# Two residual blocks on one core: projection, norm and transposes chained per block of 128 tokens

## What is computed

```python
h = rmsnorm(x, norm_g)            # before each L1 layer
proj = h @ w_in
...
x = x + u @ w_o                   # end of each L1 layer
# second kind, twice:
h = rmsnorm_2(x, g_mix[l]);  proj = h @ w_in;  ...;  x = x + merged @ w_out[l]
h = rmsnorm_2(x, g_mlp[l]);  up = square(relu(h @ w_up[l]));  x = x + up @ w_down[l]
# at the end
return rmsnorm_2(x, g_final)
```

## Time and profile before

| | us |
|---|---|
| median of 3 runs (3376.45 to 3382.3) | 3376.96 |
| the profiled execution's own time | 3382.91 |
| span of that execution, first to last instruction | 3381.1 |
| PE matmul busy | 3251.9 (96%) |
| DVE / ACT / POOL busy | 1437.8 / 820.0 / 1821.1 |
| mean granted TensorE clock | 0.986 |

### The profile page before, as it was taken

One profiled execution on the slowest core, in us unless ns is written; L12 is line 12 of the kernel. 1 busy time (PEld: TensorE's weight loads), 2 busy tenths in 40 slices (PEclk: granted clock), 3 DMA queues, 4 the chain that ended last, 5 costly groups with the idle time before them and its releaser, 6 DMA issues.

```text
span 3381.1 us, 47060 instructions
## 1 busy us (share of the span) xinstructions
PE 3251.9 (96%) x15456; PEld 2691.9 (80%) x15456; DVE 1437.8 (43%) x2325; ACT 820.0 (24%) x1773; POOL 1821.1 (54%) x1028
## 2 busy tenths in 40 slices
PE   5998999998998999999999999999899999999998
PEld 4877888886777888878887887888788888878887
DVE  7777462117776642126666112111166662121011
ACT  4554332014554331022222002101122220021020
POOL 3444455663444555655455665666554555656664
PEclk9999999999999999999999999999999999999999
DMA  3222222222221222232222222222222222222322
GB/s 106 75 89 67 69 75 81 98 98 63 87 87 57 76 73 89 98 102 84 75 84 78 90 96 88 94 99 95 83 84 84 75 83 87 99 87 94 99 93 99
DMA packets 87983, 290.54 MB, mean 86 GB/s; under 512 B 12833, under 2 KB 13537, under 8 KB 87921
## 3 DMA queue, kind: packets, MB, share of 16 engines
q1 hardware_dynamic: 75024, 273.12, 24.3%
q10 hardware_dynamic: 12896, 16.64, 1.8%
HBM read 275.00 MB, written 2.10 MB: 82 GB/s over the span
## 4 chain that ended last, share of the span: by engine, by line
PE 87%; DVE 7%; issue 3%; ACT 1%; ACTq 1%; DVEq 0%; DMA 0%
PE bank L556 27%; PE bank L558 27%; PE bank L557 27%; PE bank L624 1%; DVE xq L1416 1%; PE bank L742 1%; PE bank L605 1%; PE bank L653 1%; DVE k_hi L1347 1%; ACTq L1032 1%; PE bank L775 1%; DVE xk L1416 1%; DVE xn L1356 0%; DVE xk L1412 0%; PE bank L715 0%
## 5 line engine op out<-in xcount | busy, mean ns | idle before, releaser
L537 POOL TENSOR_SCALAR w_hi<-raw 128x1024 fp32r<-128x1024 f32 x512 | 560.6, 1095 | 1493.7 <-DMA raw<-in_w_in 1026.9
L540 POOL TENSOR_TENSOR w_lo<-raw,w_hi 128x1024 fp32r<-128x1024 f32 x512 | 1260.4, 2462 | 42.7
L556 PE MATMUL bank<-h_lo,w_hi 128*128 128x512 f32 x2816 | 1118.4, 397 | 0.6 <-DVE h_lo L1359 0.3
L558 PE MATMUL bank<-h_hi,w_hi 128*128 128x512 f32 x2816 | 1099.9, 391 | 0.0
L557 PE MATMUL bank<-h_hi,w_lo 128*128 128x512 f32 x2816 | 1098.7, 390 | 0.0
L558 PEld LDWEIGHTS bank<-h_hi,w_hi 128*128 128x128 f32 x2816 | 530.4, 188 | 113.2
L556 PEld LDWEIGHTS bank<-h_lo,w_hi 128*128 128x128 f32 x2816 | 531.4, 189 | 108.8 <-issue 2.5
L557 PEld LDWEIGHTS bank<-h_hi,w_lo 128*128 128x128 f32 x2816 | 531.6, 189 | 106.0
L1373 DVE TENSOR_TENSOR x<-x,bank 128x512 f32 x64 | 44.0, 688 | 458.1 <-PE bank L558 458.1
L556 PE MATMUL bank<-w_lo,up_hi 128*128 128x512 f32 x512 | 199.2, 389 | 0.0
L557 PE MATMUL bank<-w_hi,up_lo 128*128 128x512 f32 x512 | 199.2, 389 | 0.0
(11 more groups left out here) (297 smaller groups left out, 4520.1 us busy)
## 6 DMA issues: line engine op xcount, KB each, us to landing
raw<-in_w_in SPq DMA_DIRECT2D x288, 512.0 KB, 3.3
raw<-in_w_up SPq DMA_DIRECT2D x64, 512.0 KB, 3.3
raw<-in_w_down SPq DMA_DIRECT2D x64, 512.0 KB, 3.2
raw<-in_w_out_a SPq DMA_DIRECT2D x16, 512.0 KB, 3.2
raw<-in_w_out_b SPq DMA_DIRECT2D x16, 512.0 KB, 3.3
raw<-in_w_o SPq DMA_DIRECT2D x16, 512.0 KB, 3.2
raw<-in_p_ret SPq DMA_DIRECT2D x16, 512.0 KB, 3.3
raw<-in_p_sb SPq DMA_DIRECT2D x16, 512.0 KB, 3.3
```

Of the source, the lines that this page charges most:

```text
L537: nc.gpsimd.tensor_scalar(m.w_hi[:, slot], m.raw[:, slot], 1.0, 0.0, ALU.mult, ALU.add).then_inc(s["w_step"], 1)
L540: nc.gpsimd.tensor_tensor(m.w_lo[:, slot], m.raw[:, slot], m.w_hi[:, slot].bitcast(F32), ALU.subtract).then_inc(s["split"], 1)
L556: nc.tensor.matmul(dst, hi, rhs_lo, start=first, stop=False, **more)
L558: return nc.tensor.matmul(dst, hi, rhs_hi, start=False, stop=last, **more)
```

## The change

1. `project` keeps the panels' order for all but the last three (`HELD = 3`) and does these three sorted by block: block 0 of the three panels, block 1, and so on. The two column halves are written out, and in the second half of a projection that a norm follows, PE transposes block 0 (8 transposes) behind the matmuls of block 1, and block 1 behind those of block 2. `used` for the three panels is given only in the last block.
2. `first_panels` replaces the first two gemms of the next stage: transposes of block 2; first panel, tokens 0 to 255; transposes of block 3; second panel, tokens 0 to 255; then tokens 256 to 511 of both. Matmuls have 256 moving columns there, 96 in place of 48.
3. The gain is now multiplied in along the row: DVE's `normalised(b)` is a `scalar_tensor_tensor` of `x`, the root and `g_row` (128x1024, a 512 KB broadcast load for each norm). `h_high` and `h_low` work on one block of tokens, 8 steps of 128x512 as before. `xn` moves away from `u_hi`/`u_lo`.
4. The norm stands at the end of a loop turn instead of the start on ACT and DVE, so `layer_parameters` and the rotation tables of L2 are now issued behind the norm. PE's turn begins with `first_panels`.
5. At the start SP loads `x` without waiting, and the norm of the input goes ahead of the sine and cosine, the parameters and the masks.
6. PE's loops over `R_HEADS` and over the two MLP halves are partly written out, with the same work.
7. After the last projection PE still transposes all four blocks and ACT and DVE still split them, though nothing reads that.

```diff
+HELD = 3
-        place = Region(nc, o_u, o_rest)
+        place = Region(nc, o_u + 2 * tile, o_rest)
         self.xn = place.put("xn", [P, TB, D])
@@ tensor
+            def first_panels():
+                slots = [(at.n.get("panel", 0) + i) % RING for i in range(2)]
+                banks = [acc[(at.n.get("acc", 0) + i) % 2] for i in range(2)]
...
+                early, late = slice(0, 2 * P), slice(2 * P, S)
+                turn_block(2)
+                pe.wait_ge(s["split"], at.at("panel", 1))
+                pe.wait_ge(acc_free[at.n.get("acc", 0) % 2], at.at("acc", 2, div=2))
+                pe.wait_ge(s["h_ready"], at.at("norm", times=KT) + TB)
+                half(0, early)
+                turn_block(3)
+                pe.wait_ge(s["split"], at.at("panel", 2))
+                pe.wait_ge(acc_free[(at.n.get("acc", 0) + 1) % 2], at.at("acc", 3, div=2))
+                half(1, early)
+                pe.wait_ge(s["h_ready"], at.at("norm", times=KT) + KT)
+                at.add("norm")
+                for i in range(2):
+                    half(i, late).then_inc(s["used"], 1)
...
+            def project(x_hi, x_lo, tiles, ready, before, last):
+                count = tiles // 2
...
+                for q in range(count - HELD):
+                    pe.wait_ge(s["split"], at.at("panel", q + 1))
                     pe.wait_ge(s[ready], before + (2 * q + 2))
                     for b in range(TB):
                         if q == 0:
                             pe.wait_ge(s["x_done"], at.at("xb", times=TB) + (TB + b + 1))
+                        mm = part(q, b)
                     mm.then_inc(s["used"], 1)
+                for b in range(TB):
+                    for q in range(count - HELD, count):
+                        if b == 0:
+                            pe.wait_ge(s["split"], at.at("panel", q + 1))
+                            pe.wait_ge(s[ready], before + (2 * q + 2))
+                        mm = part(q, b)
+                        if b == TB - 1:
+                            mm.then_inc(s["used"], 1)
+                    if b < TB - 1:
+                        mm.then_inc(s["xb_done"], 1)
+                    if last and b in (1, 2):
+                        turn_block(b - 1)
...
+            def turn_block(b):
+                pe.wait_ge(s["xn_ready"], at.at("norm", times=TB) + (b + 1))
+                if b == 1:
+                    misc_bank()
+                elif b > 1:
+                    pe.wait_ge(s["h_ready"], at.at("norm", times=KT) + (1, 4)[b - 2])
+                for j in range(2):
                     for k in range(TB):
+                        o = (j * TB + k) * P
+                        mm = nc.tensor.transpose(turned[b][j][:, k * P:k * P + P], m.xn[:, b, o:o + P], m.ident[:])
                     mm.then_inc(s["xT_done"], 1)
@@ scalar
+            def norm(gain):
+                act.wait_ge(s["x_done"], at.at("proj", times=KT) + 1)
+                act.dma_start(m.g_row[:], gain.to_broadcast([P, D])).then_inc(s["gain_in"], 16)
...
+                for b in range(TB):
+                    act.wait_ge(s["x_done"], at.at("proj", times=KT) + (TB + b + 1))
+                    second_half_root(b)
+                    if b:
+                        h_high(b - 1)
+                h_high(TB - 1)
...
@@ vector
+            def normalised(b):
+                dve.wait_ge(s["rms_ready"], at.at("norm", times=TB) + (b + 1))
+                stt(m.xn[:, b], m.x[:, b], m.sm[:, 4 + b:5 + b], m.g_row[:], ALU.mult,
+                    ALU.mult).then_inc(s["xn_ready"], 1)
...
+            def add_and_norm(tiles):
+                add_half(0, tiles)
+                at.add("panel", tiles // 2)
+                dve.wait_ge(s["gain_in"], at.at("norm", 1, times=16))
+                for b in range(TB):
+                    add_block(1, b)
+                    normalised(b)
+                    if b:
+                        h_low(b - 1)
+                h_low(TB - 1)
```

More of the change, by code:

```diff
@@ L596, in project @@
+                at.add("panel", count)
                 at.add("xb")
@@ L832, in project_merged @@
             def project_merged():
[L833 to L838, removed]
+                for c in range(2):
+                    project(m.u_hi, m.u_lo, KT, "u_ready", at.at("merge", -1, times=KT) + 1, c == 1)
             pe.wait_ge(s["const_in"], 16 * 2)
-            pe.wait_ge(s["masks_ready"], 5)
+            turn_block(0)
+            turn_block(1)
             with at.loop(DEPTH, panel=PANELS_L1, acc=PANELS_L1 - PANELS_D, xb=2, norm=1, layer=1, merge=1,
                          a=A_HEADS, pair=B_HEADS // 2, misc=PE_MISC_L1):
-                norm()
-                at.add("norm")
-                gemm(m.h_hi, m.h_lo, fresh=True)
-                h_gemm()
+                first_panels()
+                pe.wait_ge(s["masks_ready"], 5)
                 group_sum(0, 0)
@@ L904, in _, with attention_turn @@
                          merge=1, r=R_HEADS, half=2, misc=PE_MISC_L2):
-                norm()
-                at.add("norm")
-                with at.loop(R_HEADS, panel=12, acc=12, r=1, misc=5):
-                    gemm(m.h_hi, m.h_lo, fresh=True)
-                    h_gemm()
+                def attention_turn(first):
+                    if first:
+                        first_panels()
+                    else:
+                        h_gemm()
+                        h_gemm()
                     h_gemm()
@@ L991, in inv_sqrt, with h_high @@
                 activation(dst, dst, ACT.Exp, scale=-0.5).then_inc(ready, 1)
-            def sums_of_squares():
-                halves = m.x[:].rearrange("p b (c d) -> p b c d", c=2)
+            def h_high(b):
+                for j in range(2):
+                    act.wait_ge(s["xT_done"], at.at("norm", times=KT) + (2 * b + j + 1))
+                    activation(m.h_hi[:, j * TB:j * TB + TB, b * P:b * P + P],
+                               turned[b][j][:].rearrange("p (k t) -> p k t", t=P), ACT.Copy).then_inc(s["h_hi_ready"], 1)
@@ new lines, in norm, with norm_of_input @@
+                    if b:
+                        h_high(b - 1)
+                h_high(TB - 1)
+                at.add("norm")
+            def norm_of_input():
+                for b in range(TB):
+                    act.wait_ge(x_in[b], 16)
+                    first_half_squares(b)
+                    own(activation(m.sm[:, 80 + b:81 + b], m.sm[:, b:b + 1], ACT.Identity, bias=m.col[:, 2:3],
+                                   scale=1.0 / D))
+                    second_half_root(b)
+                    if b > 1:
+                        h_high(b - 2)
+                h_high(TB - 2)
+                h_high(TB - 1)
@@ L1814, in _ @@
                 merge()
-                add_to_x(KT)
-                norm()
-                with at.loop(2, panel=PANELS_UP + PANELS_DOWN, acc=16, up=16, proj4=2, own=16) as f:
+                add_and_norm(KT)
+                for f in range(2):
                     with at.loop(4, panel=4, acc=4, up=4, own=4) as n:
```

212 lines of the change are left out of this document (104 added, 108 removed).

## The result

| | before | after |
|---|---|---|
| median us (9 runs each on one chip) | 3378.24 | 3396.16 |
| ratio, 95% interval | | 1.0040 [1.0027, 1.0054] |
| span of the profiled execution | 3381.1 | 3400.4 |
| PE matmul busy | 3251.9 | 3267.6 |

A forecast was written before the change was run, and what follows sets the result against it. PE is busy 96%, so only its idle time can be won. 10.5 - 8.7 - 2.4 - 0.5 + 8.0 + 2.5 - 0.6 - 3.4 = 5.4 us saved, giving 3371.7; range 3358 to 3386.

The forecast's parts named there:

- The slower side: Rival: the clock falls at each of 11 short waits of PE, 18.7 us in place of 3.4; 3387, chance 0.18.
- Start: Kernel start: DVE's angle chain ends at 15.96, the first transpose follows 1.3 later, not at 29.2; 2.5 us saved.
- Held panels: Second column half of four short projections: PE waits 0.8 and 2.1 us for late panels; 2.9 each, 11.6 lost.
- Straight seams: Three projection ends outside loop turns: transposes, norm and first two gemms go from 20.3 to 16.8 us; 3.5 saved each.
- Second loop turn: Seam at 2437: 9.4 us saved, less 1.0 for code fetch and 0.4 for the lock, keeps 8.0.
- the fetch: Top of PE's loop turn: PE's own code arrives late, between 0 and 3.96 us, taken as 1.0.
- First loop turn: Parameters now stand behind the norm, so `sq_k` starts at 26.9 where it was 26.2; 0.5 to 0.7 us lost.
- Lock at `xn(3)`: Block 3's norm at seams: POOL's split may block DVE, PE waits 1.3 or 0; 0.8 each, 2.4 us lost.
- Clock: Behind four held-panel waits: PE's clock drops to 1.2 GHz half the time, 1.7 us each; 3.4 lost.
- End: Behind the last projection: final stores or useless transposes and splits take 8.9 to 9.9 us, before 8.9; 0.6 lost.

The follow-up runs named there:

- the repeat: The changed kernel itself run once more, unaltered, beside the last experiments, against the kernel before: ratio 1.0027 [1.0011, 1.0042].

## Why the prediction was wrong, point by point

Forecast 3371.7 with a range to 3386; measured about 3392 by the ratio. The slower side had 0.18, and for another reason. In the profiled executions the terms below come to some 13 lost where I had 5.4 saved: 10.8 of the difference are the start, 7.7 the first loop turn and 6.2 the missing term, and the seams gave some back.

- **Start, +2.5: the step that failed.** I took DVE's chain to end at 15.96 as in the earlier trace rows, that is, I costed SP's missing wait at nothing. The edit sends the 2 MB of `x` out beside three small loads, and I worked that out for no queue. The first exponential came at 78.25 for 69.92, so the start lost 8.3. With that line restored the first exponential is 8.0 earlier than before (69.92 to 61.89), so the new order is worth more than the 2.5; the line takes back 16.4. Had I priced it, the sum would have been 11 lost, on the slower side. (The terms for `sq_q` add up to 40.4 to 42.4, not to 42.6; that changes nothing.)
- **Held panels, 2.9 each: right.** 3.2 to 3.6, at the places named, none in `w_down`. The sum of 11.6 was 13.3. Their removal brought 18 with what follows from them.
- **Straight seams, 3.5 each: right**, 4.0, but by two errors: the transposes cost 0.10 and not 0.165, 2.1 less a seam, and the second panel, which I took as hidden, made PE wait 1.0. Another 0.5 a seam is not accounted for.
- **Missing term: `rk_lo`**, 3.2 and 3.0. I counted when both panels are complete, not when the first is. Before, the old distance of 5.5 covered DVE's work on it. I had named no work queued behind `first_panels` in the second kind of layer. The 2.8 by which the chain starts later would have cost 0.4 alone; the rest is that it takes 17.4 for 14.7.
- **Second loop turn, 8.0: right in kind**, 26.26 to 16.2 is 10.0. Of the fetch that I took at 1.0 there is at most 0.5: PE's only `issue` in after, 0.51, stands at this turn, 4.3 behind the projection's last matmul, and the repeat has 0.92 there. The queue of 64 entries (the Trainium skill, TensorE: Matmul & The Clock Gate, first table), from which I had drawn 0, fits only in part; whether these are fetches is not shown.
- **First loop turn, -0.5: too small.** The seam itself won 9.2 (26.15 to 15.38 + 1.6) and the held panels took 3.25. `sql_q` then took 6.8 where there was none, and the 1.7 for `k_lo` behind it went away. From the projection's last matmul to the first of the gate rows it is 36.2 with the 1.6, for 35.5 before; with the held panels PE is thus 3.9 late there, where I had 0.5 to 0.7. The two stages around the turn are 8.2 longer in the profiled executions (43.3 to 46.0, 263.1 to 268.6). Of the 4.3 that lie behind the first gate row the clock can explain 3.4, as it stood at one half for 10.3 us there and for 3.4 before. I had seen the chain through the parameters, but gave DVE's splits of `sq_q` their free duration; they took 2.57 and 1.41 beside POOL, not 0.43 and 0.69. The loads were not what came late: the last had landed at 795.74, 14.8 behind the projection's end, where my count gives 16.2.
- **Lock at `xn(3)`, -2.4: right in size, half right in kind.** That the two operations come within half a microsecond was right, and the full price, where DVE loses, is 1.8 for my 1.3. I had not thought of POOL as the loser. In the changed kernel DVE lost only at the first loop turn, 1.79, and POOL at the three straight seams, 3 x 1.0 = 3.1; in the repeat DVE lost at one straight seam too, 1.83.
- **Clock, -3.4: right for what it was for.** Behind the held panels' waits the granted clock fell to one half (1.2 GHz) in two of the four projections, for 3.4 and 6.9 us in after and for 3.4 and 3.4 in the repeat: 5.1 and 3.4 lost. The total is another matter, as falls elsewhere went and came: one half for 99 us in after, 80 in the repeat, and 92 before.
- **End, -0.6: wrong in sign**, it won 0.7: from the last `w_down` projection's first matmul to the end it is 95.4 for 96.1.

## What to carry over

Before a wait in a DMA queue is dropped, ask which small load it kept ahead: bytes issued in another queue can delay it, and what starts 5 us late may run into work that blocks it. Where two operations that share a lock start within half a microsecond, price both orders, since either may lose. Hold buffers to the end of a stage only where something starts with that end, and give a moved operation its duration beside whatever shares its port, not its free one. When two products are finished together, the one that used to be early may have had a consumer that needed it early.

## What the runs showed of the hardware

- DVE beside POOL's split: TENSOR_SCALAR 128x512 from SBUF 0.43 alone, 2.44 to 2.58 blocked; a chain of 19 operations of that shape 10.5 us or 21.5. Operations with a bank as input kept 0.68.
- POOL loses as well: its TENSOR_TENSOR of 128x1024 took 2.4, and 3.3 to 3.5 where DVE's operation had started 0.05 us or more ahead.
- Three loads of 256, 64 and 4 KB, issued from ACT's queue by 1.7 us, have landed at 4.40 to 4.51 where the loads of `x` wait for them, and at 9.55 with 2 MB of `x` issued by SP from 0.75 on.
- PE's wait of 2.1 to 2.2 us for DVE's queue in the second kind of layer came 5 times in one execution of the kernel before, 3 and 2 times in two of the changed kernel, 5 with `HELD = 2`, and none in two of the others. The low clock followed it in all 3 cases of the changed kernel's first profile and in 3 of the 5 of the kernel before. Its cause is open. That it makes part of the scatter (3380.8 to 3402.2 us in the nine runs of after) is likely, and not shown.
